# Delta stage of a two-block model: the inverse's turns moved to VectorE, its last two levels on narrow operands, q's norm moved into the output's norm

## What is computed

```python
q = _l2norm(q) * (A_HEAD_K ** -0.5)        # 8 heads of 128
k = _l2norm(k)
...
m = jnp.where(strict, jnp.einsum("bhnid,bhnjd->bhnij", k_beta, k) * decay, 0.0)
uw = lax.linalg.triangular_solve(m + eye, rhs, left_side=True, lower=True, unit_diagonal=True)
...
def step(state, inp):
    v_new = u_c - jnp.einsum("bhcd,bhdv->bhcv", w_c, state)
    o_c = jnp.einsum("bhcd,bhdv->bhcv", qd, state) + jnp.einsum("bhcj,bhjv->bhcv", a_c, v_new)
    state = state * dec[..., None, None] + jnp.einsum("bhcd,bhcv->bhdv", ke, v_new)
    return state, o_c
...
o = rmsnorm(o, out_norm_w) * jax.nn.silu(z.reshape(bsz, seq, A_HEADS, A_HEAD_V))
```

## Time and profile before

| what | value |
|---|---|
| median of 3 runs | 1932.68 us |
| profiled execution, its time | 1932.87 us |
| profiled execution, its span | 1931.2 us |
| mean granted clock of TensorE | 0.987 |
| TensorE busy | 1853.0 us, 96% |
| VectorE busy | 1201.0 us, 62% |
| ScalarE busy | 850.3 us, 44% |
| GpSimd busy | 34.3 us, 2% |
| DMA moved | 163.28 MB, mean 85 GB/s |

### The profile page before, as it was taken

The page is one execution under the profiler, slowest core; times in us unless marked ns, Lnnn a source line. Parts: engine busy times, 40 slices in busy tenths (PEclk is TensorE's granted clock), DMA queues, the critical chain, the costliest instruction groups (busy, mean ns, idle before and its releaser), DMA issues.

```text
span 1931.2 us, 24636 instructions
## 1 busy us (share of the span) xinstructions
PE 1853.0 (96%) x8566; PEld 1471.8 (76%) x8566; DVE 1201.0 (62%) x1899; ACT 850.3 (44%) x1360; POOL 34.3 (2%) x64
## 2 busy tenths in 40 slices
PE   9999999879999999998888899999999999899997
PEld 6888888757888888887666778888887777677875
DVE  7777777745777763356656567767533588665444
ACT  6444444424444442256666544434322455543222
POOL 1000000000000000000000000000000100000000
PEclk9999999989999999999999899999999999999999
DMA  6411111102222232143322132222321311122221
GB/s 206 134 54 58 60 56 33 63 26 87 98 87 98 89 112 103 45 136 93 90 80 71 55 120 93 92 98 76 130 94 59 102 34 66 61 98 87 98 78 64
DMA packets 44825, 163.28 MB, mean 85 GB/s; under 512 B 5873, under 2 KB 6148, under 8 KB 44768
## 3 DMA queue, kind: packets, MB, share of 16 engines
q1 hardware_dynamic: 39872, 148.00, 22.5%
q0 software_dynamic: 4464, 14.47, 2.7%
q10 hardware_dynamic: 432, 0.07, 0.0%
HBM read 155.89 MB, written 6.63 MB: 84 GB/s over the span
## 4 chain that ended last, share of the span: by engine, by line
PE 87%; DVE 5%; ACT 5%; issue 3%; DMA 0%; DVEq 0%; SPq 0%; ACTq 0%
PE acc L543 21%; PE acc L544 21%; PE acc L545 21%; PE acc L567 8%; PE pb L682 2%; PE pc L697 2%; DVE wsplit L1577 1%; PE pa L955 1%; PE pd L967 1%; PE pd L686 1%; PE pa L644 1%; PE pa L663 1%; PE pd L905 1%; ACT wsplit L1087 1%; ACT prob L1392 1%
## 5 line engine op out<-in xcount | busy, mean ns | idle before, releaser
L543 PE MATMUL acc<-xhi,wsplit 128*128 128x512 f32 x1200 | 497.9, 415 | 13.3 <-DVE wsplit L1577 7.4
L1087 ACT ACTIVATE wsplit<-wraw 128x1024 fp32r<-128x1024 f32 (+1 forms) x252 | 275.3, 1097 | 457.4 <-PE acc L545 421.7
L544 PE MATMUL acc<-xlo,wsplit 128*128 128x512 f32 x1200 | 476.2, 397 | 0.0
L545 PE MATMUL acc<-xhi,wsplit 128*128 128x512 f32 x1200 | 475.9, 397 | 0.0
L1577 DVE TENSOR_TENSOR wsplit<-wraw,wsplit 128x1024 fp32r<-128x1024 f32 (+1 forms) x252 | 320.1, 1274 | 126.7 <-ACT wsplit L1087 124.9
L543 PEld LDWEIGHTS acc<-xhi,wsplit 128*128 128x128 f32 x1200 | 226.6, 189 | 74.8 <-issue 11.8
L544 PEld LDWEIGHTS acc<-xlo,wsplit 128*128 128x128 f32 x1200 | 226.9, 189 | 55.4 <-issue 4.3
L545 PEld LDWEIGHTS acc<-xhi,wsplit 128*128 128x128 f32 x1200 | 226.3, 189 | 54.9
L567 PE MATMUL acc<-xhi,wsplit 128*128 128x512 f32 x464 | 158.4, 409 | 0.0
L545 PE MATMUL acc<-hid_hi,wsplit 128*128 128x512 f32 x352 | 139.5, 396 | 0.0
L544 PE MATMUL acc<-hid_lo,wsplit 128*128 128x512 f32 x352 | 139.5, 396 | 0.0
(11 more groups left out here) (340 smaller groups left out, 2800.9 us busy)
## 6 DMA issues: line engine op xcount, KB each, us to landing
wraw<-w SPq DMA_DIRECT2D x220, 512.0 KB, 3.2
wraw<-w SPq DMA_DIRECT2D x32, 704.0 KB, 4.1
bias_dram<-ext_dram POOLq DMA_DIRECT2D x1, 4096.0 KB, 20.4
bias<-bias_dram POOLq DMA_DIRECT2D x16, 256.0 KB, 3.0
at_ks<-at_ks SPq DMA_DIRECT2D x16, 256.0 KB, 2.9
crow<-row_dram POOLq DMA_DIRECT2D x8, 256.0 KB, 3.8
brow<-row_dram POOLq DMA_DIRECT2D x8, 256.0 KB, 4.4
outT<-h SPq DMA_DIRECT2D x8, 256.0 KB, 2.1
```

What stands on the lines that cost most here:

```text
L543: mm(out, whi[:, k, :], a[:, x_at + k, :], start=(k == first), stop=False)
L544: mm(out, whi[:, k, :], b[:, x_at + k, :], start=False, stop=False)
L545: m = mm(out, wlo[:, k, :], a[:, x_at + k, :], start=False, stop=(k == last))
L1087: A(split(s, j, 0), raw(s, j), ACT.Copy).then_inc(w_hi_ready, 1)
```

## The change

On VectorE the turn of a block-diagonal tile is done in 32x32 blocks by its own transpose instruction: behind each add to `tn` of levels 0 to 3 it writes `tt`, and at the head's start it writes `tn` from the first `tt`. TensorE's turns (`first_turn`, L686) and VectorE's copies from `pd` go. At level 4 (blocks of 32) X takes 96 columns of `gd` and the two even 32-column blocks of `tn` as moving side, the mask becomes two negated copies of 32 partitions into a new tile `xm32`, the join moves 32 columns, and its result is copied into `tn` and turned in two small pieces into `tt`. At level 5 X and join have 64 by 64 columns, and the result is copied into the corner of `tt`. Of q only the silu is kept: its norm is no longer computed on its own. Instead the squares of q, scaled, are added by VectorE to the squares of `o` (`with_q`), so that the sum of both carries the epsilon of q's norm, and the sum of `o` waits for that addition. ScalarE squares q later (`square_q`), its Ln and Exp of the norms work on k alone, and silu writes q into `kq` directly. The pieces of fill are handed out anew: `AFTER_X`, `AFTER_JOIN`, and 20 pieces behind the sum of `o` in one.

```diff
-            AFTER_X, AFTER_JOIN = [5, 5, 4, 4, 4, 4], [5, 5, 4, 4, 4, 0]
+            AFTER_X, AFTER_JOIN = [5, 5, 5, 5, 3, 3], [5, 5, 4, 4, 3, 1]
...
-            AFTER_GRAM = 10
+            AFTER_GRAM = 20
...
+            nc.gpsimd.memset(xm32[:], 0.0).then_inc(ev("zeroed"), 1)
...
-                m = mm(pa[:, half, :], ones, sq[:, half, :], start=True, stop=True)
-                if half == 1:
-                    m.then_inc(ev("qk_sums"), 1)
+            def sums_of_k(i):
+                pe.wait_ge(ev("k_squared"), i + 1)
+                mm(pa[:, 1, :], ones, sq[:, 1, :], start=True, stop=True).then_inc(ev("k_sums"), 1)
...
-            def first_turn(i):
-                pe.wait_ge(ev("tt_ready"), i * (NL + 1) + 1)
-                pe.wait_ge(ev("o_ln"), i + 1)
-                for t in range(NC):
-                    m = turn(pd[:, t * P:t * P + P], tt[:, t, :], ident)
-                m.then_inc(ev("tn_turned"), 1)
...
                     for t in range(NC):
-                        m = mm(pb[:, t * P:t * P + P], gd[:, t, 0, :], tn[:, t, :], start=True, stop=True)
+                        if n < NL - 2:
+                            m = mm(pb[:, t * P:t * P + P], gd[:, t, 0, :], tn[:, t, :], start=True, stop=True)
+                        elif n == NL - 2:
+                            m = mm(pb[0:96, t * 64:t * 64 + 64], gd[:, t, 0, 32:P], even_blocks(tn[:, t, :]), start=True, stop=True)
+                        else:
+                            m = mm(pb[0:64, t * 64:t * 64 + 64], gd[:, t, 0, 64:P], tn[:, t, 0:64], start=True, stop=True)
                     m.then_inc(ev("x_done"), 1)
-                    if n > 0:
-                        for t in range(NC):
-                            m = turn(pd[:, t * P:t * P + P], tn[:, t, :], ident)
-                        m.then_inc(ev("tn_turned"), 1)
...
+                        elif n == NL - 2:
+                            m = mm(pc[0:96, t * 32:t * 32 + 32], tt[:, t, 32:P], xm32[:, t, :], start=True, stop=True)
                         else:
-                            m = mm(pd[:, t * P:t * P + P], xm[:, t, :], tt[:, t, :], start=True, stop=True)
+                            m = mm(pd[0:64, t * 64:t * 64 + 64], xm[:, t, 0:64], tt[:, t, 64:P], start=True, stop=True)
...
-                        if t == 1 and not last:
-                            sums_of(i + 1, 0)
...
-                pe.wait_ge(ev("o_squared"), i + 1)
+                pe.wait_ge(ev("o_with_q"), i + 1)
                 mm(pd[:], ones, sq_o[:], start=True, stop=True).then_inc(ev("o_sums"), 1)
...
+            def square_q(i):
+                act.wait_ge(ev("qkv_silu"), i * 3 + 1)
+                if not (isinstance(i, int) and i == 0):
+                    act.wait_ge(ev("o_with_q"), i)
+                A(chunks(sq[:, 0, :]), kq[:, :, 1, :], ACT.Square, scale=EPS ** 0.5 * P).then_inc(ev("q_squared"), 1)
...
-                A(rqk[:], pa[:], ACT.Ln, bias=eps_d).then_inc(ev("rqk_ln"), 1)
+                A(rqk[:], pa[:, 1, :], ACT.Ln, bias=eps_d).then_inc(ev("rqk_ln"), 1)
...
                 if not last:
                     bv_of(i + 1)
                     ecrow_of(i + 1)
+                    square_q(i + 1)
...
+            nc.vector.memset(epst[:, 1:2], EPS * EPS * P).then_inc(ev("eps_ready"), 1)
...
-                stt(kq[:, :, 1, :], chunks(ys[:, 0, :]), float(P) ** -0.5, chunks(rqk[:, 0, :]), ALU.mult, ALU.mult
-                    ).then_inc(ev("qn_ready"), 1)
...
                     ).then_inc(ev("decay_masked"), 1)
+                if after is not None:
+                    with_q(after)
                 dve.wait_ge(ev("decay_masked"), i + 1)
                 dve.wait_ge(ev("gram_done"), i + 1)
...
+                dve.wait_ge(ev("tt_ready"), i * (NL + 1) + 1)
+                turn_blocks(tn, tt).then_inc(ev("tn_ready"), 1)
+
+            def turn_blocks(out, of):
+                return nc.vector.transpose(out[:].rearrange("p t q -> p (t q)"), of[:].rearrange("p t q -> p (t q)"))
+
+            def with_q(i):
+                dve.wait_ge(ev("o_squared"), i + 1)
+                dve.wait_ge(ev("q_squared"), i + 1)
+                tt_(sq_o[:], sq_o[:], sq[:, 0, :], ALU.add).then_inc(ev("o_with_q"), 1)
...
-                    tt_(xm[:], chunks(pb[:]), over_chunks(cst[:, C_LEV + n, :]), ALU.mult).then_inc(ev("xm_ready"), 1)
-                    if n > 0:
-                        dve.wait_ge(ev("tn_turned"), i * NL + (n + 1))
-                        nc.vector.tensor_copy(tt[:], chunks(pd[:])).then_inc(ev("tt_ready"), 1)
+                    if n < NL - 2:
+                        tt_(xm[:], chunks(pb[:]), over_chunks(cst[:, C_LEV + n, :]), ALU.mult).then_inc(ev("xm_ready"), 1)
+                    elif n == NL - 2:
+                        x = pb[0:96, 0:4 * 64].rearrange("p (t c) -> p t c", t=NC)
+                        ts_(xm32[32:64], x[0:32, :, 0:32], -1.0, None, ALU.mult)
+                        ts_(xm32[96:P], x[64:96, :, 32:64], -1.0, None, ALU.mult).then_inc(ev("xm_ready"), 1)
+                    else:
+                        x = pb[0:64, 0:4 * 64].rearrange("p (t c) -> p t c", t=NC)
+                        ts_(xm[64:P, :, 0:64], x, -1.0, None, ALU.mult).then_inc(ev("xm_ready"), 1)
                     between(2 * n)
                     dve.wait_ge(ev("join_done"), i * NL + (n + 1))
-                    if n < NL - 1:
+                    if n < NL - 2:
                         tt_(tn[:], tn[:], chunks(pc[:]), ALU.add).then_inc(ev("tn_ready"), 1)
+                        dve.wait_ge(ev("tn_ready"), i * NL + (n + 2))
+                        turn_blocks(tt, tn).then_inc(ev("tt_ready"), 1)
+                    elif n == NL - 2:
+                        x = pc[0:96, 0:4 * 32].rearrange("p (t c) -> p t c", t=NC)
+                        nc.vector.tensor_copy(tn[32:64, :, 0:32], x[0:32]).then_inc(ev("tn_ready"), 1)
+                        nc.vector.transpose(tt[0:32, :, 32:64], x[0:32])
+                        nc.vector.transpose(tt[64:96, :, 96:P], x[64:96]).then_inc(ev("tt_ready"), 1)
                     else:
-                        dve.wait_ge(ev("tt_ready"), i * (NL + 1) + (n + 1))
-                        tt_(tt[:], tt[:], chunks(pd[:]), ALU.add).then_inc(ev("tt_ready"), 1)
+                        x = pd[0:64, 0:4 * 64].rearrange("p (t c) -> p t c", t=NC)
+                        nc.vector.tensor_copy(tt[0:64, :, 64:P], x).then_inc(ev("tt_ready"), 1)
                     between(2 * n + 1)
...
                     gram(i + 1, i)
+                else:
+                    with_q(i)
```

More of the change, by code:

```diff
@@ L186, in build @@
         sq = r.sb("sq", [P, 2, S])
-        rqk = r.sb("rqk", [P, 2, S])
+        rqk = r.sb("rqk", [P, S])
+        r.at += 3 * P * 4
         kq = r.sb("kq", [P, NC, 2, P])
@@ L199, in build @@
         xm = r.sb("xm", [P, NC, P])
+        xm32 = r.sb("xm32", [P, NC, 32])
         kend = r.sb("kend", [P, NC, P])
@@ L345, in chunks, with even_blocks @@
             return ap.rearrange("p (t q) -> p t q", t=NC)
+        def even_blocks(ap):
+            return ap.rearrange("p (g a c) -> p g a c", g=2, a=2)[:, :, 0, :]
         def over_chunks(ap):
@@ L757, in delta @@
                         fill(AFTER_GRAM)
+                        fill(2 * 3 * KD - done[0])
                     elif done[0] < 3 * KD:
                         fill(3 * KD - done[0])
[L760 to L765, removed]
+            sums_of_k(0)
             strips(s, 0, (0, 1), 0, 3 * KD)
@@ L1168, in silu, with square_k @@
                 act.wait_ge(ev("conv_done"), i * 3 + (3 + j))
[L1169 to L1173, removed]
-                act.wait_ge(ev("qkv_silu"), i * 3 + 5)
-                A(sq[:, 1, :], ys[:, 1, :], ACT.Square).then_inc(ev("qk_squared"), 1)
+                if j == 1 and not (isinstance(i, int) and i < 0):
+                    act.wait_ge(ev("gram_done"), i + 1)
+                    act.wait_ge(ev("qe_ready"), i + 1)
+                    act.wait_ge(ev("q_squared"), i + 1)
+                A(kq[:, :, 1, :] if j == 1 else ys[:, j - 1, :], chunks(ys[:, 0, :]) if j == 1 else ys[:, j - 1, :], ACT.Silu
+                  ).then_inc(ev("qkv_silu"), 1)
+            def square_k(i):
+                act.wait_ge(ev("qkv_silu"), i * 3 + 5)
+                A(sq[:, 1, :], ys[:, 1, :], ACT.Square).then_inc(ev("k_squared"), 1)
+            def square_q(i):
[3 more added lines that the diff above has]
+                A(chunks(sq[:, 0, :]), kq[:, :, 1, :], ACT.Square, scale=EPS ** 0.5 * P).then_inc(ev("q_squared"), 1)
             act.wait_ge(ev("gate_pe"), at(GATE_PE, "gates_turned"))
@@ L1194, in _, with k_norms @@
             silu(-1, 2)
[L1195 removed]
+            square_q(0)
+            square_k(-1)
             tables("natural_log_exp_and_others")
             conv_newest(3, 0, -1)
[L1199 to L1202 removed]
+            def k_norms(i):
+                act.wait_ge(ev("k_sums"), i + 1)
+                A(rqk[:], pa[:, 1, :], ACT.Ln, bias=eps_d).then_inc(ev("rqk_ln"), 1)
```

(5 more changed lines are left out.)

47 lines of the change are left out of this document (22 added, 25 removed).

## The result

The changed kernel takes 1914.74 us (median of 4 runs, 1914.14 to 1916.21), the kernel before 1932.36 us (4 runs): ratio 0.9911, 95% interval 0.9893 to 0.9928. That is 0.9% faster. The forecast was 1912, the range 1900 to 1925. The profiled execution of after took 1914.14 us, span 1912.5 (before: 1931.2).

What follows compares the result with a forecast made beforehand. Levels were taken as bound nearly alike by TensorE and the chain through VectorE. Six loop heads -12.0, head 6 -3.3, head 7 -4.3, ahead of head 0 -1.3: -20.9 from 1932.9 gives 1912 us, range 1900 to 1925.

Steps and rivals of the forecast that it cites:

- v to state product: `vn` behind tap and cast: Ahead of the first state product: ScalarE's tap, cast and `vn` end 1.65 us behind L736, +0.7 a loop head.
- sum of o waits for the addition: L754 waits for VectorE's addition of q's squares, queued behind `low` and the 128x1024 mask: +1.0 a loop head.
- sum of o to next X(0): Behind the sum of o, TensorE's first turn of a head falls out; VectorE's successor stays hidden: -0.4 a loop head.
- head 6: Delta stage, head 6: neither the cast ahead of `vn` nor the `low` ahead of the mask, so -3.3 us.
- head 7: Last head, little fill, the bare chain: levels save 5.0, the bare addition costs 0.7, so -4.3 us.
- the two new waits: TensorE idle ahead of the sum of o, +1.0, and ahead of the first state product, +0.7, each loop head.
- half pace: Rival, VectorE's turn: it lasts 1.22 us, +1.7 in seven heads, total 1924 us; chance 0.10.
- L736 comes at 7.6 where it was at 9.06: -1.4: Levels 4 and 5 made narrow: first v (L736) comes 7.6 us after X(4), saving 1.4 a loop head.
- only that wait's rest is won: -0.4: Between L728 and L734: dropping q's sum (L644) wins only the remaining wait after `rr`, -0.4 a loop head.
- The new waits do not bind: Rival: cast and mask find room earlier, no +0.7 and +1.0 in six heads, total 1902 us; chance 0.13.
- Narrow matmuls cost by moving columns: Rival, levels 4 and 5: joins shorter by 0.5 and 0.27 us, 0.8 a head, total 1905 us; chance 0.07.
- The three rivals that needed a slow turn: VectorE's turn: half pace, 1924 us (0.10); nets out at T near 1.5, 1933 (0.04); slower, 1962 (0.06).

Runs made afterwards that it cites:

- the run with the swapped gaps: Two pairs of VectorE fillers change places, against the kernel with addition and last piece moved earlier and decayed q in level 0: 1901.20 us, ratio 0.9835.

## Why the prediction was right, and where its steps were not

| step (us, loop head unless said) | predicted | measured |
|---|---|---|
| level 0 | 0 | 0 |
| level 1 | -0.4 | -0.32 |
| levels 2 and 3 | -1.05 | -0.95 |
| levels 4 and 5 | -1.4 | -1.02 |
| v to state product: `vn` behind tap and cast | +0.7 | +0.62 |
| sum of q gone | -0.4 | -0.26 |
| chunks 1 to 3 | 0 | +0.13 |
| sum of o waits for the addition | +1.0 | +0.93 |
| sum of o to next X(0) | -0.4 | -0.34 |
| **period** (the steps give -1.95, rounded up) | **-2.0** | **-1.21** |
| six heads | -12.0 | -7.3 |
| head 6 | -3.3 | -3.2 |
| head 7 | -4.3 | -4.6 |
| ahead of head 0 | -1.3 | -1.3 |
| behind the delta stage | 0 | -2.3 |

Head 6 is counted, as the prediction laid it, up to X of level 1 in head 7, whose level 0 grew from 6.07 to 7.00 us; by the starts of X(0) head 6 won 4.1 and head 7 3.7.

**Right.** Every step that was priced had the sign and place that were foreseen, the two new waits too, and the turn's price: 0.69 was taken from the copy it replaces, 0.71 measured, which rules out half pace and all that lay beyond it. By the Trainium skill ("Vector Engine (DVE) Microarchitecture Reference", The reshape front-end and per-opcode configuration) it keeps the pace of one element per cycle and lane. The row agrees, 0.71 beside the copy's 0.68.

**Mis-sized: "L736 comes at 7.6 where it was at 9.06: -1.4".** This is the step that failed; it came at 8.04. Against X(4) the prediction had the halves of `xm32` done at 1.81, the join at 1.87, X(5) at 3.4, `low` at 4.9, `xm` at 5.25, the join at 5.3, `take` at 7.2; after has 1.93, 2.07, 3.63, 5.17, 5.62, 5.86 and 7.66. The chain is the one that I drew. The narrow joins start 0.14 and 0.24 us behind their operand where I took some 0.05, and VectorE's small operations do not overlap where each begins on another partition than the one ahead. Here is its timeline of after, last full level to the last copy:

```profile
158.28 0.71 DVE L1739 STREAM_TRANSPOSE tt<-tn 128x512 f32<-128x512 f32 x1
158.91 0.71 DVE L1649 SCALAR_TENSOR_TENSOR ys<-tmp,vec,ys 128x510 f32<-128x510 f32 x1
159.65 0.28 DVE L1781 TENSOR_SCALAR xm<-pb 32x128 f32<-32x128 f32 x1
159.94 0.29 DVE L1782 TENSOR_SCALAR xm<-pb 32x128 f32<-32x128 f32 x1
...
161.26 0.28 DVE L1794 COPY tn<-pc 32x128 f32<-32x128 f32 x1 [0.25 <-PE pc L700]
161.58 0.30 DVE L1795 STREAM_TRANSPOSE tt<-pc 32x128 f32<-32x128 f32 x1
161.89 0.32 DVE L1796 STREAM_TRANSPOSE tt<-pc 32x128 f32<-32x128 f32 x1
162.24 1.23 DVE L1585 TENSOR_TENSOR wsplit<-wraw,wsplit 128x1024 fp32r<-128x1024 f32 x1
163.50 0.42 DVE L1785 TENSOR_SCALAR xm<-pb 64x256 f32<-64x256 f32 x1
165.27 0.69 DVE L1639 TENSOR_TENSOR tmp<-acc,rstd 128x512 f32<-128x512 f32 x1 [1.36 <-PE acc L574]
165.88 0.41 DVE L1799 COPY tt<-pd 64x256 f32<-64x256 f32 x1
```

The tap starts 0.08 before the turn ends, as full-width rows do, and so does the last copy, which begins on partition 0 like the `take` ahead of it; in between the next starts 0.01 to 0.04 after the end. VectorE's queue is what the last levels wait for, and the run with the swapped gaps showed how to shorten it. Added up along this chain, the miss of 0.44 is +0.27 from the two hand-overs and +0.40 from VectorE's operations, less 0.23 because the join's result (0.86 behind its start where I took 0.99) and the `take` came sooner. The narrow groups themselves were no dearer than the 0.72 that I took: 0.58 to 0.70.

**Mis-sized: "only that wait's rest is won: -0.4"** measured 0.26, and chunks 1 to 3, booked at nothing, took 0.13 more; with q's norm restored they take 6.58 of the 6.69. What each of these comes from was not followed further.

**The total came closer than its steps.** The delta stage won 16.4 us of the 20.9, and the stretch behind it gave 2.3 that no step had; its first 20 us had the granted clock 0.83 instead of 0.74, and that this is the cause is read from the rows, not tested. With 18.7 off the span the profiled execution landed 2 us over the forecast. So much of that nearness is luck.

**The rivals.** *The new waits do not bind* fell: they bind in every loop head. *Narrow matmuls cost by moving columns* fell: L683 and L700 have 64 and 32 moving columns and hold TensorE 0.70 and 0.69 us, to the next dense record. The three rivals that needed a slow turn fell with its price.

## What to carry to other kernels

Price a wait that moves with what stands behind it on every queue, and look then for the one handed-out piece of fill that causes it: one matmul of 0.23 us moved ahead of a join gave 9 us, more than half of what the whole change had given. Where two queues hold the same step, each edit alone gains next to nothing and both together much more (level 0 fell from 4.87 by 0.1, 0.1 and 0.6 us here), so follow an edit that did nothing to the next row that ends the wait before you drop it. A part that removes work, like q's norm, can still cost time when it hangs a wait behind a long operation; undo the parts one by one.

## What was not expected of the hardware

Eight matmuls with up to 128 moving columns hold TensorE, start to the start of the next dense record, 0.80 to 0.91 us at 128 stationary columns, 0.70 at 96 and 0.58 to 0.61 at 64. At 96 it makes no difference whether 64 or 32 columns move (0.70 and 0.69), so that is the stationary width's doing, and it is less than proportional. By the Trainium skill ("TensorE: Matmul & The Clock Gate", LDWEIGHTS (loading the stationary operand)) the load goes by the stationary columns; its formula gives, as an estimate, 0.107, 0.080 and 0.053 us at these widths. The runs have 0.100 to 0.114, 0.087 and 0.073 to 0.076 a record: the direction agrees, and from 128 to 64 columns 0.02 to 0.04 us are saved where the formula has 0.054.

VectorE's operations that begin on different partitions follow each other without overlap (161.58 and 161.89 above), while two that begin on the same one overlap by 0.08 us (165.27 and 165.88). The Trainium skill ("VectorE: DVE Perf Modes", Two Vector instructions with no wait between them) has an instruction held until the earlier ones end when its operands start in another group of 32 partitions. The rows agree.

That the clock in the first 20 us behind the delta stage takes one of two means, 0.74 or 0.83, with no edit that goes along with either, was a surprise too. In both cases TensorE comes from head 7's bare chain, with idle time between its products; why one execution gets the clock sooner stays open.
